# One-core fp32 kernel of two transformer blocks: modulation tiles as row sums on VectorE, exponentials moved behind splits and copies, part of an output projection inside the attention, four stores

## The chip, the cores and the metric

One Trainium2 chip; the program uses one of its cores. The metric is the device time of one execution in microseconds (us); lower is better.

## The reference

Two blocks run one after the other on 256 tokens of width 1024, all in fp32. The first has two layers: norm, an input projection, a convolution, a pooling mixer and a sparse attention, an output projection, a gated add of a side input. The second has two layers on the same tokens and, in its first layer, on 256 context tokens beside them (so 512 columns in layer 0, 256 in layer 1):

```python
mod = jax.nn.silu(c) @ w_ada[layer] + b_ada[layer]
sh1, sc1, g1, sh2, sc2, g2 = jnp.split(mod[:, None, :], 6, axis=-1)
modc = jax.nn.silu(c_ctx) @ w_ada[layer] + b_ada[layer]
...
u = modulate(rmsnorm_2(x, norm_mix_g[layer]), sh1, sc1) @ w_in[layer]
...
gla_lat, gla_ctx = gla_mixer(lat[:6], cpar[:6], rope, ...)
...
x = x + g1 * (jnp.concatenate([gla_lat, sc_lat, na_lat], axis=-1) @ w_out[layer])
h = modulate(rmsnorm_2(x, norm_ffn_g[layer]), sh2, sc2)
x = x + g2 * conv_ffn(h, ffn_w_up[layer], ffn_conv_w[layer], ffn_conv_b[layer], ffn_w_down[layer])
```

The modulation (mod and modc) is a product of two vectors, one for the tokens and one for the context, with a 1024 x 6144 matrix in each layer. It needs nothing but the inputs and can be computed at any time before its use.

## The kernel before, in words

The engines are TensorE (PE), VectorE (DVE), ScalarE (ACT), GpSimd (POOL) and SyncE (SP). Each runs its own instruction list, written out by hand, and waits on semaphores for the others.

**Weights.** All weights come as units of 128 x 1024 (512 KB) in the order that `stream()` writes. SP (line 434) loads them into a ring of four slots, RAWB; a slot is loaded again when its unit has been used up. An fp32 product is made of three products of operands split in a high and a low part: ACT copies a unit to WHI (line 1299, the helper through which every ACT instruction goes), DVE subtracts it from the unit to get WLO (line 1832). The split ring has three slots and runs two units ahead (AHEAD). `rest()` and `split_to()` are the places in the ACT and DVE lists where the next split stands. The activations are split too, into NHI and NLO.

**A tile** is 128 output channels: `fm` issues 8 slabs of three matmuls (lines 561 to 563) over 512 or 256 columns. `native` tiles (line 577) skip the split and multiply RAWB in fp32; in block 1 these are the tiles from NATIVE_FROM on, which stand beside its attention. `tm` units (lines 622 to 624) make token-major values V, copied from PSUM by ACT's `values`.

**Block 1** (0 to 400 us): per layer, values, tile 0, then tiles 1 to 22. DVE's `divide` (line 1887) scales a tile by the token norm, ACT adds the bias into Z, PE rotates (line 813), DVE applies the ropes (lines 2007 to 2012).

**Block 2**: per layer an input projection of 17 tiles and 8 value units, in the order 4 tiles, 4 value units, 13 tiles; beside it ropes and gates (GQ: exponential and logarithm on ACT; line 2475 on DVE), cumulative sums on PE (line 1080) behind tile 6, `cross_exponentials` on ACT at tile 8, the gated mixer's matmuls. Then a softmax attention by items (one pair of heads and 128 queries each): scores (line 1256), row maximum on DVE, exponential on ACT, transposes (line 736), values (line 1265). Then the output projection (8 tiles), statistics (line 697), `modulate` on DVE (GM, TB and NLO), the feed-forward: 44 tiles up, 8 tiles of three units down.

**The modulation** is cut in 24 tiles of 512 outputs, four units each, 12 for each layer. A "row" tile is computed by PE (`rows`, line 531, into a bank of 32 partitions), copied by ACT, turned into columns by four small matmuls (`columns`, line 542) and biased by DVE. A "dot" tile is computed by DVE alone (`dot`, line 1924): one instruction multiplies a unit with the broadcast vector CREP and sums along the row, per column of the modulation; units of tiles that also serve the context need two. Before, tiles 0 to 10 are rows: 0 to 3 in block 1 (ROWS1), 4 beside block 2's first tiles (ROWS2), 5 to 9 in layer 0's attention (BESIDE_ROWS), 10 behind the output projection's statistics; tiles 11 to 23 are dots in layer 0's feed-forward.

## Time and profile before

| what | value |
|---|---|
| median of 3 runs | 1489.95 us (1489.83 to 1494.48) |
| profiled execution | 1486.99 us, its span 1485.2 us |
| PE busy | 1402.2 us (94%) |
| VectorE busy | 987.8 us (67%) |
| ScalarE busy | 710.4 us (48%) |
| block 1 | 0 to some 400 us |
| block 2, layer 0; layer 1 | to 1061 us; to 1485 us |

Busy time is the time in which an engine executes an instruction. A timeline row gives start, length, engine, line, operation, what is written and read, how many instructions, and in brackets the idle time before it and what ended it.
### The profile page before, as it was taken

To read this page: it belongs to the slowest core of one execution; us is meant where nothing else is said; L and a number is where in the kernel's file an instruction comes from. 1 tells how busy PE (TensorE), PEld (TensorE's weight loads), DVE (VectorE), ACT (ScalarE), POOL (GpSimd) and SP (SyncE) were. 2 spreads that over 40 slices of the span, in tenths; PEclk is the share of its full clock that TensorE was granted. 3 is DMA by queue.
4 is the path that set the end of the run, shared out by engine and by line. 5 is a ranking of instruction groups with operands and counts; after the bars stand their busy time and mean duration, and the time that the engine had idled before them with its cause. 6 is when DMAs were issued, how large, how long until landed. Compare 5 with 4: busy or idle time off the path is not lost.

```text
span 1485.2 us, 22067 instructions
## 1 busy us (share of the span) xinstructions
PE 1402.2 (94%) x8641; PEld 1201.1 (81%) x8641; DVE 987.8 (67%) x1907; ACT 710.4 (48%) x1195; POOL 47.4 (3%) x66
## 2 busy tenths in 40 slices
PE   6999998998999999999999999999899988899997
PEld 4777897778977886577888888888788867899997
DVE  5597685977743385645798897665533655788854
ACT  5537565366534632633444444312344636566642
POOL 0000000000000012000000000000000210000000
PEclk9999999999999999998999999999899999999998
DMA  6633556334452221642345445567233331365552
GB/s 242 227 131 125 159 184 201 129 100 159 140 168 85 67 95 53 230 168 100 128 156 169 158 156 175 172 221 243 96 112 100 105 99 56 128 196 177 183 185 81
DMA packets 61752, 217.48 MB, mean 146 GB/s; under 512 B 6960, under 2 KB 9008, under 8 KB 61392
## 3 DMA queue, kind: packets, MB, share of 16 engines
q1 hardware_dynamic: 59152, 205.55, 42.1%
q0 software_dynamic: 2352, 10.52, 2.1%
q8 instruction: 69, 1.13, 0.3%
q14 instruction: 35, 0.29, 0.1%
q10 hardware_dynamic: 144, 0.00, 0.0%
HBM read 214.99 MB, written 1.05 MB: 145 GB/s over the span
## 4 chain that ended last, share of the span: by engine, by line
PE 80%; DVE 8%; ACT 7%; issue 3%; DMA 1%; DVEq 0%; ACTq 0%
PE bank L561 19%; PE bank L563 19%; PE bank L562 19%; PE bank L577 3%; ACT WHI L1299 2%; DVE WLO L1832 2%; PE bank L1137 1%; ACT L1299 1%; PE bank L622 1%; PE bank L623 1%; PE bank L624 1%; PE bank L531 1%; PE bank L736 1%; PE bank L599 1%; PE bank L1265 1%
## 5 line engine op out<-in xcount | busy, mean ns | idle before, releaser
L1832 DVE TENSOR_TENSOR WLO<-RAWB,WHI 128x1024 fp32r<-128x1024 f32 (+1 forms) x280 | 333.5, 1193 | 271.5 <-ACT WHI L1299 270.3
L561 PE MATMUL bank<-NHI,WHI 128*128 128x256 f32 (+1 forms) x1440 | 481.7, 335 | 15.8 <-DVE WLO L1832 8.6
L562 PE MATMUL bank<-NLO,WHI 128*128 128x256 f32 (+1 forms) x1440 | 474.0, 329 | 0.0
L563 PE MATMUL bank<-NHI,WLO 128*128 128x256 f32 (+1 forms) x1440 | 474.0, 329 | 0.0
L1299 ACT ACTIVATE WHI<-RAWB 128x1024 fp32r<-128x1024 f32 (+1 forms) x280 | 287.5, 1029 | 194.7 <-PE bank L563 131.5
L561 PEld LDWEIGHTS bank<-NHI,WHI 128*128 128x128 f32 x1440 | 275.7, 191 | 51.9 <-issue 14.7
L562 PEld LDWEIGHTS bank<-NLO,WHI 128*128 128x128 f32 x1440 | 275.9, 192 | 25.5 <-issue 2.2
L563 PEld LDWEIGHTS bank<-NHI,WLO 128*128 128x128 f32 x1440 | 275.5, 191 | 24.2
L1299 ACT ACTIVATE CF<-bank,PRM 128x512 f32<-128x512 f32 (+1 forms) x88 | 59.1, 671 | 178.7 <-PE bank L563 175.9
L561 PE MATMUL bank<-HHI,WHI 128*128 128x512 f32 (+1 forms) x352 | 119.3, 339 | 0.0
L563 PE MATMUL bank<-HHI,WLO 128*128 128x512 f32 (+1 forms) x352 | 119.2, 339 | 0.0
L562 PE MATMUL bank<-HLO,WHI 128*128 128x512 f32 (+1 forms) x352 | 119.2, 339 | 0.0
L1924 DVE CUSTOM_DVE_ANT_0 DP<-RAWB,CREP,PRM 128x1024 f32<-128x1024 f32 x72 | 92.3, 1282 | 3.5
L2559 DVE SCALAR_TENSOR_TENSOR CF<-bank,PRM,CF 128x510 f32<-128x510 f32 (+1 forms) x88 | 54.1, 615 | 50.7 <-ACT CF L1299 49.2
L577 PE MATMUL bank<-Y,RAWB 128*128 128x256 f32 x320 | 75.1, 389 | 0.0
L561 PEld LDWEIGHTS bank<-HHI,WHI 128*128 128x128 f32 x352 | 66.3, 188 | 8.3 <-DVE WLO L1832 0.2
L562 PEld LDWEIGHTS bank<-HLO,WHI 128*128 128x128 f32 x352 | 66.3, 188 | 8.1
L563 PEld LDWEIGHTS bank<-HHI,WLO 128*128 128x128 f32 x352 | 66.3, 188 | 8.1
L1299 ACT ACTIVATE L<-L,ST 128x256 f32<-128x256 f32 (+2 forms) x100 | 50.2, 518 | 39.3 <-DVE ST L1942 16.4
L577 PEld LDWEIGHTS bank<-Y,RAWB 128*128 128x128 f32 x320 | 60.6, 193 | 9.8 <-issue 1.7
L1299 ACT ACTIVATE ZB<-bank 128x512 f32<-128x512 f32 (+1 forms) x34 | 17.7, 520 | 95.0 <-PE bank L563 94.9
L622 PE MATMUL bank<-WHI,NHI 128*128 128x384 f32 (+1 forms) x128 | 47.9, 375 | 12.4 <-DVE WLO L1832 9.3
(319 smaller groups left out, 1928.4 us busy)
## 6 DMA issues: line engine op xcount, KB each, us to landing
RAWB<-in_ws SPq DMA_DIRECT2D x364, 512.0 KB, 3.4
RAWB<-in_ws SPq DMA_DIRECT2D x32, 384.0 KB, 3.5
NB<-in_nab POOLq DMA_DIRECT2D x12, 256.0 KB, 3.7
K<-in_c POOLq DMA_DIRECT2D x2, 896.0 KB, 4.7
K<-in_c POOLq DMA_DIRECT2D x1, 1344.0 KB, 7.9
X<-in_xt SPq DMA_DIRECT2D x4, 256.0 KB, 5.8
X<-in_xt POOLq DMA_DIRECT2D x1, 1024.0 KB, 6.5
CREP<-in_crep POOLq DMA_DIRECT2D x1, 1024.0 KB, 5.0
```

Of the source, the lines that this page charges most:

```text
L531: ins = nc.tensor.matmul(bank[b][g:g + 32, :], CV2[:, s, 8 - 2 * at:40 - 2 * at], RAWB[:, u % RAW, (s % 2) * 512:(s % 2 + 1) * 512], start ...
L561: nc.tensor.matmul(o, hi[:, w], xh, start=(i == 0), stop=False)
L562: nc.tensor.matmul(o, hi[:, w], xl, start=False, stop=False)
L563: ins = nc.tensor.matmul(o, lo[:, w], xh, start=False, stop=(i == slabs - 1))
L577: ins = nc.tensor.matmul(bank[b][:, 0:T], RAWB[:, u % RAW, s * P:(s + 1) * P], Y1[:, s, :], start=(s == 0), stop=(s == KS - 1))
L599: nc.tensor.matmul(o, hi[:, w], xh, start=(i == 0), stop=False)
L622: nc.tensor.matmul(o, xh, hi[:, c], start=(s == 0), stop=False)
L623: nc.tensor.matmul(o, xl, hi[:, c], start=False, stop=False)
L1299: return nc.scalar.activation(out, in_, func, **kw)
L1832: V.tensor_tensor(WLO[:, k % SPL, 0:w], RAWB[:, u % RAW, 0:w], WHI[:, k % SPL, 0:w].bitcast(F32), ALU.subtract).then_inc(S("lo_ready"), 1)
L1924: V.tensor_tensor_reduce(out=DP[:], in0=RAWB[:, u % RAW, :], in1=CREP[:, c, :], scale=1.0, scalar=prm_col(f"bada{l}", at), op0=ALU.mult, o ...
L2559: V.scalar_tensor_tensor(y[:, :, 1:], b[:, :, :-1], prm_col(f"fw{l}", j), y[:, :, 1:], ALU.mult, ALU.add).then_inc(S("dve_chain"), 1)
```

## The change

- Block 1: the two kb tiles are native too; the row units of tile 1 go to tile 2, and the division of tile 2 stands ahead of the split there.
- Modulation tiles 5 to 10 become dots. Twenty of their units go beside layer 0's input projection, in the numbers of DOTS_PROJ behind each tile or value unit, with a broadcast vector and a scratch tile of their own (CREP1, DP1); the other four shift the rest. The rows, copies, columns and additions of these tiles go.
- ACT copies the second half of the values and makes one more split before the exponential of the gates, and takes the logarithm a tile later; it makes one more split before `cross_exponentials`.
- Five of the eight slabs of the output projection's first tile are issued inside the softmax attention, in bank 3 (FIRST_OUT_AT).
- `modulate` computes GM before the statistics, and scales and splits by halves of 256 columns.
- The result is stored in four pieces.

```diff
-NATIVE_FROM = Z1["pin"]
+NATIVE_FROM = Z1["kb"]
...
-ROWS1 = (1, 4, 7, 10)
+ROWS1 = (2, 4, 7, 10)
...
-BESIDE_ROWS = 5
 ROWS2 = (0, 2)
-DOT_TILES = range(11, 24)
+FIRST_OUT_AT = ({7: (0,), 8: (1,), 9: (2,), 10: (3,), 11: (4,)}, {6: (0, 1), 7: (2, 3), 8: (4,)})
+DOT_TILES = range(5, 24)
+DOTS_FIRST = 20
+DOTS_PROJ = (1, 1, 1, 2, 2, 1, 2, 2, 2, 2, 2, 2)
 DOTS_UP = [m for m in range(5, 2 * FT) if m % 3]
-DOTS_DOWN = (4, 4, 4, 4, 4, 4, 2, 0)
+DOTS_DOWN = (5, 5, 5, 5, 4, 4, 2, 0)
...
+            dots(DOTS_PROJ[i] if l == 0 else 0)
             rows(2 if l == 0 and i in ROWS2 else 0)
-        add([2 * VW] * 4 + [UNIT] * (NZ2 - NFIRST))
-        rows(BESIDE_ROWS * ROW_U if l == 0 else 0)
+        for j, width in enumerate([2 * VW] * 4 + [UNIT] * (NZ2 - NFIRST)):
+            add([width])
+            dots(DOTS_PROJ[NFIRST + j] if l == 0 and NFIRST + j < len(DOTS_PROJ) else 0)
...
-            sp.wait_ge(S("x_new"), KS * (DEPTH + 2))
-            sp.dma_start(out, X[:, :, 0:T]).then_inc(S("stored"), 16)
-            sp.wait_ge(S("stored"), 16)
+            for k in range(0, KS, 2):
+                sp.wait_ge(S("x_new"), KS * (DEPTH + 1) + k + 2)
+                sp.dma_start(out[:, k:k + 2, :], X[:, k:k + 2, 0:T]).then_inc(S("stored"), 16)
+            sp.wait_ge(S("stored"), 16 * KS // 2)
...
+                if l == 0:
+                    pool.dma_start(CREP1[:], crep).then_inc(S("ld_crep"), 16)
...
+                if l == 0:
+                    pool.wait_ge(S("dot_summed"), DOTTED[DOTS_FIRST])
...
+                first_unit = []
+
+                def first_out(s):
+
+                    if s == 0:
+                        pe.wait_ge(*held[3])
+                        first_unit.append(unit())
+                    (hi, lo), (xh, xl) = first_unit[0], rhs(s)
+                    w, o = slice(s * P, (s + 1) * P), bank[3][:, 0:n]
+                    nc.tensor.matmul(o, hi[:, w], xh, start=(s == 0), stop=False)
+                    nc.tensor.matmul(o, hi[:, w], xl, start=False, stop=False)
+                    return nc.tensor.matmul(o, lo[:, w], xh, start=False, stop=(s == KS - 1))
+
                 def end_of_gated(i):
 
                     if i == 0:
                         output_means()
                     if i == 2:
                         output_scales()
-                    h = i - 3
-                    if uc and 0 <= h < 2 * BESIDE_ROWS:
-                        rows(3, 4 * (h % 2), 4 * (h % 2) + 4, h // 2, BESIDE_ROWS)
+                    if i == min(FIRST_OUT_AT[l]):
+                        pe.wait_ge(S("y_split"), me.nth("y_split", 5))
+                    for s in FIRST_OUT_AT[l].get(i, ()):
+                        first_out(s)
...
+                me.from_bank_3()
+                me.next_tile()
                 attention(items2(uc), score2, L2, lambda e: (4 + e, 0), pv2, uc, end_of_gated)
-                pe.wait_ge(S("y_split"), me.nth("y_split", 5))
-                me.from_bank_0()
+                for s in range(5, KS):
+                    pe.wait_ge(S("y_split"), me.nth("y_split"))
+                    ins = first_out(s)
+                ins.then_inc(S("unit_done"), 1)
+                read_by(3, "wo_freed")
                 for m in range(KS):
-                    fm(KS, n, rhs, "wo_freed", "y_split" if m == 0 else None, 5)
-                    if uc and m == 1:
-                        columns(3, BESIDE_ROWS)
+                    if m > 0:
+                        fm(KS, n, rhs, "wo_freed")
                     stats_behind(m, n, SQ2)
-                if uc:
-                    rows(5)
                 spread_scales("r_tok", "r_spread", n // P)
-                held[4] = (S("t_ready"), me.nth("t_ready", KS))
+                held[4] = (S("t_ready"), me.nth("t_ready", KS * seqs))
                 fm_side_by_side(AHEAD, n, rhs, "up_freed", "x_split")
...
+                    A(CREP1[:], CREP1[:], ACT.Silu).then_inc(S("crep_ready"), 1)
...
+                values(1)
+                split_to(me.u + 1 + AHEAD)
                 act.wait_ge(S("act_chain"), me.nth("act_chain", 4))
                 A(GTA, GTA, ACT.Exp, scale=-1.0).then_inc(S("act_chain"), 1)
-                act.wait_ge(S("act_chain"), me.nth("act_chain"))
-                A(GTA, GTA, ACT.Ln, bias=1.0).then_inc(S("gln_ready"), 1)
-                values(1)
                 for i in range(NFIRST, NZ2):
                     tile(i)
+                    if i == NFIRST:
+                        split_to(me.u + 1 + AHEAD)
+                        act.wait_ge(S("act_chain"), me.nth("act_chain"))
+                        A(GTA, GTA, ACT.Ln, bias=1.0).then_inc(S("gln_ready"), 1)
                     if i == 6:
                         fold_last_heads()
                     if i == 7:
@@ -1736,6 +1767,7 @@
                             act.wait_ge(S("b_ready"), me.nth("b_ready"))
                             A(BG[:, j, :], bank[4 + j][:]).then_inc(S("b_copied"), 1)
                     if i == 8:
+                        split_to(me.u + 1 + AHEAD)
                         cross_exponentials()
...
+                    if t == 2:
+                        divide(l, 2)
...
-                        divide(l, 2)
...
+                stats(n)
+
+                def scaled(s, c):
+
+                    w = slice(c * T, (c + 1) * T)
+                    V.scalar_tensor_tensor(TB2[:, s, w], X[:, s, w], GM[:, s, c:c + 1], bank[4][:, w],
+                                           ALU.mult, ALU.mult).then_inc(S("t_ready"), 1)
+
+                def low(s, c):
+
+                    w = slice(c * T, (c + 1) * T)
+                    dve.wait_ge(S("xh_ready"), me.nth("xh_ready"))
+                    dve.wait_ge(S("t_ready"), me.nth("t_ready"))
+                    return V.scalar_tensor_tensor(NLO[:, s, w], TB2[:, s, w], MOD[:, l, shift + s, c:c + 1],
+                                                  NHI[:, s, w].bitcast(F32), ALU.add, ALU.subtract)
+
                 for s in range(KS + 1):
                     if s in rests:
                         rest()
-                    for c in range(n // T):
-                        w = slice(c * T, (c + 1) * T)
-                        if s < KS:
-                            ins = V.scalar_tensor_tensor(TB2[:, s, w], X[:, s, w], GM[:, s, c:c + 1], bank[4][:, w], ALU.mult, ALU.mult)
                     if s < KS:
-                        ins.then_inc(S("t_ready"), 1)
+                        scaled(s, 0)
                     if s >= 1:
-                        dve.wait_ge(S("xh_ready"), me.nth("xh_ready"))
-                        dve.wait_ge(S("t_ready"), me.nth("t_ready"))
-                        for c in range(n // T):
-                            w = slice(c * T, (c + 1) * T)
-                            ins = V.scalar_tensor_tensor(NLO[:, s - 1, w], TB2[:, s - 1, w], MOD[:, l, shift + s - 1, c:c + 1],
-                                                         NHI[:, s - 1, w].bitcast(F32), ALU.add, ALU.subtract)
+                        for c in range(seqs):
+                            ins = low(s - 1, c)
                         ins.then_inc(S("x_split"), 1)
-
-            def residual(l, n, gate, units, sq, dots=(), beside=None):
+                    if s < KS and seqs == 2:
+                        scaled(s, 1)
...
+                def dots_beside(j):
+
+                    for _ in range(DOTS_PROJ[j] if l == 0 and j < len(DOTS_PROJ) else 0):
+                        dot()
+
                 for i in range(NFIRST):
                     rest()
+                    dots_beside(i)
                 if l == 0:
                     modulation(7)
                 for u in range(4):
                     rest()
+                    dots_beside(NFIRST + u)
                     if u == 1:
                         dve.wait_ge(S("ld_c2"), 16 * 2 * (l + 1))
                         for t in range(3):
                             rope(t)
                 for i in range(NFIRST, NZ2):
                     rest()
+                    dots_beside(4 + i)
+                    if l == 0 and i == 8:
+                        dve.wait_ge(S("dot_summed"), DOTTED[DOTS_FIRST])
```

Three places where the order moves. ACT's list in block 2, layer 0, from the last gate copies on (GQ are the gates, V the values, ZB a tile's copy), before:

```order
L1299 ACTIVATE GQ<-bank 128x2x192 x2
L1299 ACTIVATE WHI<-RAWB 128x1024
L1299 ACT_TABLE_LOAD
L1299 ACTIVATE GQ<-GQ 128x1536
L1299 ACT_TABLE_LOAD
L1299 ACTIVATE GQ<-GQ 128x1536
L1299 ACTIVATE V<-bank 128x384 x4
L1299 ACTIVATE WHI<-RAWB 128x1024
L1299 ACTIVATE ZB<-bank 128x512
L1299 ACTIVATE WHI<-RAWB 128x1024
```

and after:

```order
L1326 ACTIVATE GQ<-bank 128x2x192 x2
L1326 ACTIVATE WHI<-RAWB 128x1024
L1326 ACTIVATE V<-bank 128x384 x4
L1326 ACTIVATE WHI<-RAWB 128x1024
L1326 ACT_TABLE_LOAD
L1326 ACTIVATE GQ<-GQ 128x1536
L1326 ACTIVATE ZB<-bank 128x512
L1326 ACTIVATE WHI<-RAWB 128x1024
L1326 ACT_TABLE_LOAD
L1326 ACTIVATE GQ<-GQ 128x1536
L1326 ACTIVATE ZB<-bank 128x512
```

The four copies of V and a split stand ahead of the first table load, and a tile's copy and a split between the two exponential passes.

DVE's list in the same projection, two tiles of it, before:

```order
L2306 TENSOR_TENSOR ZB<-ZB,K 128x256
L2309 TENSOR_TENSOR ZB<-ZB,AM 128x256
L1832 TENSOR_TENSOR WLO<-RAWB,WHI 128x1024 x4
L2475 SCALAR_TENSOR_TENSOR GQ<-bank,GQ 128x2x192 x4
L1832 TENSOR_TENSOR WLO<-RAWB,WHI 128x1024 x3
L2332 COPY MR<-BK 128x16
L2333 COPY MR<-BK 128x2
```

and after (two units stand beside each tile; ISA rows that read RAWB are the row sums, those of 128x1 the read of their result):

```order
L1953 ISA DP,MOD<-RAWB,CREP,PRM 128x1024
L1953 ISA MOD 128x1
L1953 ISA DP,MOD<-RAWB,CREP,PRM 128x1024
L1953 ISA MOD 128x1
L2522 SCALAR_TENSOR_TENSOR GQ<-bank,GQ 128x2x192 x4
L1860 TENSOR_TENSOR WLO<-RAWB,WHI 128x1024
L1953 ISA DP,MOD<-RAWB,CREP,PRM 128x1024
L1953 ISA MOD 128x1
```

Where splits stood alone (four, the gates, three), four row sums stand between each two of them, and the gates (GQ) stand behind all that came before.

PE's list in layer 0's softmax attention, two items of it, before:

```order
L531 MATMUL bank<-RAWB,CV 32x512 x4
L736 MATMUL bank<-CST,L 128x128 x8
L1265 MATMUL bank<-PT,V 64x128 x8
L1256 MATMUL bank<-ZB 128x512 x2
L531 MATMUL bank<-RAWB,CV 32x512 x4
L736 MATMUL bank<-CST,L 128x128 x4
L1265 MATMUL bank<-PT,V 64x128 x8
L1256 MATMUL bank<-ZB 128x512 x2
L531 MATMUL bank<-RAWB,CV 32x512 x4
```

and after:

```order
L749 MATMUL bank<-CST,L 128x128 x8
L1292 MATMUL bank<-PT,V 64x128 x8
L1283 MATMUL bank<-ZB 128x512 x2
L1265 MATMUL bank<-NHI,WHI 128x512
L1266 MATMUL bank<-NLO,WHI 128x512
L1267 MATMUL bank<-NHI,WLO 128x512
L749 MATMUL bank<-CST,L 128x128 x4
L1292 MATMUL bank<-PT,V 64x128 x8
L1283 MATMUL bank<-ZB 128x512 x2
L1265 MATMUL bank<-NHI,WHI 128x512
```

The row matmuls between scores and transposes are gone, and a slab of the output projection's first tile stands in their place.

## Rows read from the trace of the kernel before

**Rows 1.** The page: busy us (share), instructions.

```profile
PE 1402.2 (94%) x8641; PEld 1201.1 (81%) x8641; DVE 987.8 (67%) x1907; ACT 710.4 (48%) x1195; POOL 47.4 (3%) x66
```

**Rows 2.** Timelines (start, length; idle before, releaser): block 1, layer 0, second projection tile.

```profile
44.74 0.42 DVE L1887 TENSOR_TENSOR Z<-bank,MS 128x256 f32<-128x256 f32 x1
...
45.76 0.70 PE L813 MATMUL bank<-Z,K 128*128 128x512 f32 x1 [2.31 <-ACT Z L1299]
```

**Rows 3.** The same place in layer 1, and the busy times around it.

```profile
231.49 1.06 ACT L1299 ACTIVATE WHI<-RAWB 128x1024 fp32r<-128x1024 f32 x1 [3.97 <-DMA RAWB<-in_ws]
...
236.03 1.22 PE L813 MATMUL bank<-Z,K 128*128 128x512 f32 x1 [3.51 <-ACT Z L1299]
...
232.00:240.00 8.00, 4.49 (x20) 3.25 (x19) 4.06 (x7) 4.87 (x8) 0.00 (x0) 0.79 0.51 169
```

**Rows 4.** By stretch, busy us (count): PE, PEld, DVE, ACT, POOL; PEclk, DMA, GB/s.

```profile
66.00:112.00 46.00, 43.91 (x273) 35.91 (x271) 42.00 (x124) 19.08 (x46) 0.92 (x1) 0.96 0.44 150
...
760.00:780.00 20.00, 20.00 (x90) 16.58 (x89) 18.52 (x25) 7.66 (x11) 0.00 (x0) 1.00 0.51 160
1300.00:1320.00 20.00, 20.00 (x169) 20.00 (x168) 17.31 (x30) 12.88 (x22) 0.00 (x0) 1.00 0.63 202
```

**Rows 5.** PE behind ScalarE's Exp, Ln: waits (total, times, longest), layer 0's row, stretch.

```profile
PE bank L561 <- ACT V L1299: 7.1, 2, 3.5
...
468.13 0.80 PE L561 MATMUL bank<-NHI,WHI 128*128 128x512 f32 x1 [3.54 <-ACT V L1299]
...
468.00:472.00 4.00, 3.87 (x10) 3.07 (x11) 1.23 (x1) 2.16 (x5) 0.00 (x0) 0.58 0.00 0
```

**Rows 6.** Block 2, layer 1: PE behind the cross exponentials, and the stretch.

```profile
1166.19 0.35 PE L561 MATMUL bank<-NHI,WHI 128*128 128x256 f32 x1 [3.62 <-DVE WLO L1832]
...
1162.00:1172.00 10.00, 6.38 (x41) 6.20 (x41) 7.14 (x19) 8.78 (x14) 0.00 (x0) 0.83 0.32 106
```

**Rows 7.** Line 1924 alone; unit loads (KB, us to landing); layer 0's input projection.

```profile
L1924 DVE CUSTOM_DVE_ANT_0 DP<-RAWB,CREP,PRM x72: 1276/1284/1287, 729.0 to 1045.1; 128x1024 f32<-128x1024 f32 x72
...
RAWB<-in_ws SPq DMA_DIRECT2D x364, 512.0 KB, 3.4
...
400.00:440.00 40.00, 38.27 (x204) 32.23 (x204) 19.34 (x40) 16.51 (x26) 3.51 (x5) 1.00 0.43 140
440.00:480.00 40.00, 36.46 (x188) 32.25 (x187) 12.54 (x21) 15.45 (x20) 0.00 (x0) 0.96 0.30 100
```

**Rows 8.** VectorE and PE in that projection: a weight split, the gates, the sums.

```profile
439.34 0.96 DVE L1832 TENSOR_TENSOR WLO<-RAWB,WHI 128x768 fp32r<-128x768 f32 x1 [5.53 <-ACT WHI L1299]
...
478.13 1.95 DVE L2475 SCALAR_TENSOR_TENSOR GQ<-bank,GQ 128x384 f32<-128x384 f32 x4
...
486.10 1.04 PE L1080 MATMUL bank<-K,GQ 128*128 128x256 f32 x5
```

**Rows 9.** Attention of layer 0, then of layer 1: PE's row matmuls, and stretches.

```profile
L531 PE MATMUL bank<-RAWB,CV 128*32 128x512 f32 x80 | 12.7, 604 | 0.0
...
600.00:638.00 38.00, 38.00 (x327) 19.16 (x325) 23.26 (x84) 24.34 (x66) 1.42 (x2) 1.00 0.83 287
...
1226.00:1230.00 4.00, 4.00 (x28) 3.03 (x26) 3.27 (x11) 3.59 (x10) 0.00 (x0) 0.61 0.06 23
```

**Rows 10.** The first tile of the output projection: PE's start, VectorE's last operand.

```profile
638.01 0.50 PE L561 MATMUL bank<-NHI,WHI 128*128 128x512 f32 x1
...
639.48 0.69 DVE L2539 TENSOR_TENSOR NLO<-OY,NHI 128x512 fp32r<-128x512 f32 x1 [5.03 <-ACT NHI L1299]
```

**Rows 11.** Between projection and feed-forward, layer 0.

```profile
686.14 3.48 PE L531 MATMUL bank<-RAWB,CV 128*32 128x512 f32 x16
...
707.78 0.50 PE L542 MATMUL bank<-CST,ROWS 128*128 128x2 f32 x4
```

**Rows 12.** The end: last scaling of VectorE; the store's GB/s in 1470 to 1486, 0.4 us each.

```profile
1476.73 3.22 DVE L2582 SCALAR_TENSOR_TENSOR X<-X,PRM,bank 128x256 f32<-128x256 f32 x8 [1.39 <-PE bank L785]
...
GB/s 0 0 0 0 0 0 0 0 0 0 0 20 0 0 0 0 0 0 0 0 0 0 0 0 0 0 0 0 269 346 351 346 346 348 348 269 0 0 0 0
```

60 lines of the change are left out of this document (27 added, 33 removed).

## Prediction

> **What bounds it now.** I read the page first: PE is busy 1402.2 of the 1485.2 us [rows 1], so all engines but PE matter only where PE waits for them, and at most 83 us can come from waits; the rest must come from PE work removed. Then PE's timeline with its idle times, place by place, and at each the engine named there; then stretches, for how full VectorE is where work is put on it, and for the granted clock. VectorE is the engine to watch: nearly full in the feed-forward of layer 0 (18.52 of 20 us, while PE never waits [rows 4]), almost empty in that layer's input projection (19.34 and 12.54 of 40 us [rows 7]). From the stretches without a PE gap I price a tile: 90 matmuls in 20 us make a 24-matmul tile 5.3 to 5.4 us with 512 columns, 169 make it 2.9 us with 256 [rows 4]. All terms are in profiled time (span 1485.2, run 1486.99 us); the median of the runs is 2.96 us above that, and I add this at the end.
>
> **Block 1, the head of each layer: -5.6.** At its second projection tile PE waits for a division on VectorE that stands behind a weight split, which waits for ScalarE, which waited for a weight unit's DMA: 2.31 us in layer 0 [rows 2], 3.51 in layer 1 after a DMA wait of 3.97 [rows 3]. The row units of tile 1 go to tile 2 and the division goes ahead of the split, so both waits should go. Layer 1's stretch also shows a clock of 0.79 over 8 us, 1.7 us lost [rows 3], most of it in the tile after the wait; I take back 1.3 of it and 0.5 of the slow rotation. The row matmuls, 1.0 us in each layer (two units, eight matmul records; 80 take 12.7 us in the attention [rows 9], so 1.3, of which 0.3 overlaps what follows), no longer hide under a wait: +1.0 twice. So -1.3 in layer 0 and -4.3 in layer 1. If a new wait for the row units' slots comes at tile 2, only -3.
>
> **The two kb tiles unsplit: -3.1.** A native tile takes PE some 0.6 us more than a split one (3.6 against 2.9 by their neighbours), +1.2 a layer, and frees VectorE of two splits of 1.22 us. VectorE is busy 42.00 of 46 us there while PE loses 2.1 us and some clock [rows 4], so I count what is freed: -2.0 in layer 0, -1.1 in layer 1. Bounds: +2.4 (nothing comes of it), -4.6.
>
> **Row sums beside layer 0's input projection: +2.4.** 20 units with two columns are 40 instructions of 1.284 us [rows 7], 1.32 apart, 51 to 53 us of VectorE. Up to tile 3 they fit in its idle time. From the split at 439.34 [rows 8] the queue is full: 13 units (34.3), seven splits (three of 0.96, four of 1.22: 7.8), the ropes (3.9), a bias (0.2) and the gates (1.95 [rows 8]) end at about 487.5, against 480.1 now. PE would come to the sums that read those gates at 486.10 [rows 8] less what the next part gives (3.54 + 1.64), at 480.9, and so waits some 6.6 us in all, part of it earlier, at the gates' banks and at splits. Half a microsecond of gaps in tile 11 goes. Waits of this size cost clock: the tile after 3.54 us ran at 0.58 for 4 us, 1.7 us lost [rows 5]; I put 1.4 here. So -5.2 + 6.6 + 1.4 - 0.4 = **+2.4**, with layer 0's gain from the Exp and Ln order in it. Behind the full queue stand GpSimd's clearing of QX and the K2 load behind one more 1 MB load; both have over 25 us until used. Bounds: -4 if splits are never late, +6 if they are late at each tile. The other eight instructions go to feed-forward tiles whose VectorE has 1.5 us in 20 free [rows 4]: 4 x 1.32 us over 40 tiles, nothing; without that cover up to +5.
>
> **Rows out of layer 0's attention: -1.6.** The five row tiles hold PE for 12.7 us there [rows 9], and PE is busy 38.00 of 38 us. But the order transpose, values, next scores, row maximum, exponential is a chain of its own, ending each item at most 1.4 us ahead of PE; without the rows it comes out only some 1.7 us shorter. Bounds: 0 (+3 if the clock falls) and -4.
>
> **Five slabs of the first output tile inside the attention: -2.5 in layer 0, 0 in layer 1.** PE starts that tile at 638.01, and the last operand is ready at 640.17 (639.48 + 0.69) [rows 10]. Of 5.4 us, only the slabs 5 to 7 remain, the last starting at about +2.2 and ending at +2.9: -2.5. The 15 matmuls of 0.23 us fit where the 12.7 us of rows were.
>
> **Columns, statistics, operand order: -3.3.** The two column groups go (five matmuls and four; four take 0.50 us [rows 11]): -1.1. The 3.48 us of row matmuls behind the statistics [rows 11] cover a Newton iteration on VectorE, which starts when the statistics end and comes out from under them: between 0 (it is as long as they are) and -3.5 (nothing waits for it); I take -0.8, near the first, as the next matmuls read its result. The gain product ahead of the statistics and the half-wise scaling: -0.6 before the feed-forward of layer 0, -0.8 in layer 1.
>
> **Layer 1's values and splits ahead of the exponentials: -7.3.** PE waits twice for the value copies behind Exp and Ln with their table loads, 7.1 us in all, 3.5 each [rows 5]. With the copies ahead layer 1's wait goes, 3.5 and 1.4 of clock: -4.9. The wait of 3.62 us behind the cross exponentials, in a stretch at clock 0.83 [rows 6], gets one more split tile (2.9 us of PE) in hand: -2.9, less 0.5 as that split now delays the exponentials: -2.4. Late next would be Ln, which the gates need five tiles later.
>
> **Stores: -2.3.** The last scaling ends at 1479.95, the kernel at 1485.2 [rows 12]: 5.25 us for 1 MB, of which 3.0 move bytes at some 350 GB/s [rows 12]; a last quarter needs 0.75 and the same 2.2 of start and end. The Trainium skill ("DMA: Bandwidth & Descriptors", "Anatomy of one DMA — SWDGE (gpsimd) path") puts a fixed cost of about 2.0 us on each DMA and so speaks against small ones; by it a 256 KB store takes 2.6 us, and four in a row would lose 6 if they queued. The row's own split, 2.2 and 3.0, agrees with the fixed part; I take it as overlapped, since scalings free a quarter every 0.8 us. By the rule without overlap the stores would be +4 and the total 1473.
>
> **Sum.** -5.6 - 3.1 + 2.4 - 1.6 - 2.5 - 3.3 - 7.3 - 2.3 = -23.3: 1463.7 profiled, **1466.7** on the median.
>
> **Rivals.**
> 1. **The ring exposes each row sum (slower).** A row-sum unit lies in one of the four weight slots until VectorE has summed it, and a load lands 3.4 us after its issue [rows 7]. If the slot of each of the 13 later units came free only as the next split wants it, each would cost that 3.4 us: +44, 1508. It becomes slower than before once VectorE's queue slips 23.3 us, that is 1.8 us per unit. Against: each tile brings three units in 6.4 us, and each load has 4.5 us or more from its slot's release to its use; 287 GB/s flowed in the attention. Chance 0.04.
> 2. **The clock takes half (smaller gain).** With rows in the attention the clock stays 1.00; layer 1's attention, without them, shows 0.61 from 1226 [rows 9], nearly the lower of TensorE's two levels. If layer 0's goes the same way over some 10 us (+4), the waits in the input projection cost 3 more of clock and the native tiles give nothing (+3): -13, 1477. The Trainium skill ("TensorE: Matmul & The Clock Gate", "HAM oscillation — how this bites in real kernels") says that a TensorE idle between bursts falls back to 1.2 GHz, a rule that speaks against taking filler matmuls out. By that rule, the trace agrees for layer 1's attention; for layer 0, whose PE stays nearly full with slabs in it, no row decides. Chance 0.22.
> 3. **VectorE keeps up (larger gain).** If the 6.6 us of waits and their clock don't appear, because row sums slip into idle time before 439, -8 more: 1459. Chance 0.12.
> 4. **Nothing to measure.** Gains on PE come back as waits at the next split; 1490 within 0.3%. Against: six of the waits end on orders that the change plainly alters. Chance 0.04.
>
> **Numbers.** The forecast has 0.58. Measurement tells 0.3%, 4.5 us. Its own bounds give 1461 to 1472; with rivals 2 and 3 inside, 1458 to 1478 leaves out rivals 1 and 4 and a little of each edge. Faster 0.92, same 0.04, slower 0.04.
>
> **What would show it.** PE busy falls by some 20 us (12.7 + 3.5 + 1.1 of rows and columns, 2.1 of clock, less 2.4 of native tiles). The waits of PE for V and Z are gone; a new one, for gates or splits, stands at about 480 to 490. VectorE is nearly full from 430 to 485. PEclk near 450 to 480 is 0.9 or above, and 1.00 in layer 0's attention; if it is below 0.8 there, rival 2. The last projection tile of layer 0 starts some 25 us late if rival 1 holds. The last store lands under 3 us after its issue; at 5 or more, the store term fails. A span of block 1 not 7 us shorter would make the first two terms wrong.

## The result, and the profile after

| what | before | changed |
|---|---|---|
| median | 1489.89 us (4 runs, 1486.07 to 1494.48) | 1468.44 us (4 runs, 1467.59 to 1475.27) |
| profiled run, its span | 1486.99 us, 1485.2 us | 1468.17 us, 1466.4 us |
| PE busy | 1402.2 us | 1389.6 us |
| VectorE busy | 987.8 us | 1041.9 us |

The ratio of the two is 0.987, with a 95% interval of 0.9845 to 0.9895: the change is faster by 1.3%, clear of the 0.3% that a measurement can tell. The profiled span fell by 18.8 us; 23.3 were forecast.

The busy times on the page of the changed kernel answer to [rows 1]:

```profile
PE 1389.6 (95%) x8497; PEld 1196.2 (82%) x8497; DVE 1041.9 (71%) x1993; ACT 709.3 (48%) x1191; POOL 48.0 (3%) x67
```

VectorE took on 54 us of work and PE gave off 12.6, not the 20 forecast (the terms written beside that 20 add up to 17.0). A slow clock counts as work here: the first matmul of one and the same tile is busy for 0.80 us in [rows 5], in a stretch at 0.58, and for 0.39 us at 464.30 below. The changed kernel's PE in block 1, at the second and third tile (timelines of layer 0, then layer 1) and the stretches behind the waits answer to [rows 2, 3]:

```profile
36.24 0.41 PE L837 MATMUL bank<-CST,Z 128*128 128x128 f32 x2 [3.58 <-ACT Z L1326]
...
45.53 0.59 PE L826 MATMUL bank<-Z,K 128*128 128x512 f32 x1
...
49.35 1.99 PE L544 MATMUL bank<-RAWB,CV 128*32 128x512 f32 x8
...
38.00:42.00 4.00, 4.00 (x26) 3.59 (x28) 0.68 (x2) 0.55 (x1) 0.00 (x0) 0.70 0.82 257
...
223.26 0.41 PE L837 MATMUL bank<-CST,Z 128*128 128x128 f32 x2 [1.99 <-ACT Z L1326]
...
226.00:230.00 4.00, 4.00 (x25) 3.02 (x25) 1.20 (x2) 0.83 (x3) 0.00 (x0) 0.74 0.68 214
```

The waits for Z at the second tile (2.31 and 3.51 us) are gone. But the wait one tile earlier, in which the row matmuls ran, is now 3.58 us without them (before, 2.20 and 0.32 with 1.06 us of rows between), and the tile behind it runs at a clock of 0.70; in layer 1 0.74, after 1.99 us. The row matmuls of tile 4 also take longer in layer 0, 1.99 us for eight records instead of 1.06. In layer 0 all this takes back more than the second tile gave.

Layer 0's input projection in the changed kernel: VectorE's list (timeline) where its queue fills and where the gates end it, ScalarE's logarithm, PE at the row units (with the weight load of their second unit), at the gates' second bank, at the first tile behind the values, and at the sums; then the whole stretch. It answers to [rows 5, 7, 8]:

```profile
436.07 0.96 DVE L1860 TENSOR_TENSOR WLO<-RAWB,WHI 128x768 fp32r<-128x768 f32 x1 [3.00 <-ACT WHI L1326]
...
481.61 1.95 DVE L2522 SCALAR_TENSOR_TENSOR GQ<-bank,GQ 128x384 f32<-128x384 f32 x4
...
475.87 1.49 ACT L1326 ACTIVATE GQ<-GQ 128x1536 f32<-128x1536 f32 x1
...
420.30 1.05 PE L544 MATMUL bank<-RAWB,CV 128*32 128x512 f32 x4 [0.80 <-DMA RAWB<-in_ws]
...
421.44 0.14 PEld L544 LDWEIGHTS bank<-RAWB,CV 128*32 128x32 f32 x4 [1.01 <-DMA RAWB<-in_ws]
...
452.37 0.91 PE L1054 MATMUL bank<-WG,ZB 17*128 17x192 f32 x4 [0.69 <-DVE AM L2342]
...
464.30 0.39 PE L574 MATMUL bank<-NHI,WHI 128*128 128x512 f32 x1
...
483.61 0.76 PE L1093 MATMUL bank<-K,GQ 128*128 128x256 f32 x2 [2.79 <-DVE GQ L2522]
...
436.00:484.00 48.00, 44.52 (x219) 39.15 (x218) 46.17 (x74) 20.10 (x27) 0.00 (x0) 0.96 0.73 232
```

VectorE is busy 46.17 of the 48 us from 436 to 484. From the split at 436.07 to the end of the gates at 483.56 are 47.5 us; the working had 48.2. The wait of 3.54 us for V is gone (no idle time at 464.30), and three new ones stand there, with a fourth of 1.01 us inside the row matmuls. PE comes to the sums at 480.82.

In layer 0's softmax attention (PE's timeline, its waits for the exponentials from 598 to 640 as total, times and longest, and the stretch), then behind it (the operands of the first tile, the statistics and the feed-forward's start), answering to [rows 9 to 11]:

```profile
604.23 0.89 PE L749 MATMUL bank<-CST,L 128*128 128x128 f32 x4 [1.34 <-ACT PT L1326]
...
PE bank L749 <- ACT PT L1326: 4.6, 4, 1.8
...
602.00:638.00 36.00, 30.68 (x245) 20.08 (x244) 22.10 (x78) 25.53 (x66) 0.43 (x1) 1.00 0.05 16
...
636.25 0.49 PE L1265 MATMUL bank<-NHI,WHI 128*128 128x512 f32 x1 [0.56 <-DVE NLO L2586]
...
680.54 2.07 PE L798 MATMUL bank<-CST,GR 128*128 128x128 f32 x8 [1.74 <-DVE GR L1882]
...
684.93 0.76 PE L612 MATMUL bank<-NHI,WHI 128*128 128x512 f32 x1 [2.32 <-DVE NLO L2292]
```

PE now waits for the attention's exponentials, its clock stays 1.00, and the DMA share falls from 0.83 to 0.05. In layer 1 the waits behind the exponentials (PE) answer to [rows 5, 6], and the end (scaling, the four stores with KB and median us to landing) to [rows 12]:

```profile
1123.49 0.39 PE L574 MATMUL bank<-NHI,WHI 128*128 128x256 f32 x1 [0.58 <-ACT V L1326]
...
1133.24 1.14 PE L1093 MATMUL bank<-K,GQ 128*128 128x256 f32 x5 [0.84 <-DVE GQ L2522]
...
1154.88 0.35 PE L574 MATMUL bank<-NHI,WHI 128*128 128x256 f32 x1 [2.02 <-DVE WLO L1860]
...
1460.15 3.22 DVE L2626 SCALAR_TENSOR_TENSOR X<-X,PRM,bank 128x256 f32<-128x256 f32 x8 [0.89 <-PE bank L798]
...
out_x<-X SPq DMA_DIRECT2D x4, 256.0 KB, 2.6
```

**The ledger.** The same PE instruction was looked up in both traces, and the shift of its start read stage by stage; the shifts add up to the 18.8 us. The last row is counted from VectorE's last scaling. Where an experiment gives a number of its own, it stands in brackets.

| stage | forecast | measured |
|---|---|---|
| first values (not touched) | 0 | -0.4 |
| head of block 1, layer 0, to behind the row matmuls of tile 4 | -1.3 | +1.0 |
| native kb tiles, layer 0 | -2.0 | -2.9 (e5: -1.8) |
| head of block 1, layer 1 | -4.3 | -2.1 |
| native kb tiles, layer 1 | -1.1 | -1.2 (e5: -1.2) |
| end of block 1 | 0 | +0.4 |
| layer 0's input projection to the attention | +2.4 | +4.1 |
| layer 0's attention, first tile, columns | -4.7 | -6.2 |
| statistics, GM, halves, second columns | -1.9 | -3.1 |
| layer 1: start and value units | -0.8 | +1.1 |
| layer 1: values, sums, cross exponentials | -7.3 | -6.0 |
| layer 1: gated part, attention, feed-forward | 0 | -1.3 |
| stores | -2.3 | -2.2 (e6: -2.2) |

Of the 6.2 us of layer 0's attention, first tile and columns, 2.8 are the attention itself (in the kernel before from 600.85 to 638.01, now from 599.71 to 634.03, with the slabs in it), 2.6 the first tile and 0.8 the columns.

### The profile page after: what moved, and what is told of

Its sections match the earlier page's. It is cut to its first block, busy times and chain, and to the rows that moved or that the text cites. A ratio compares the mean times of both kernels' runs of the same rounds, so it can differ in the third digit from the quotient of the medians.

```text
span 1466.4 us, 21897 instructions
## 1 busy us (share of the span) xinstructions
PE 1389.6 (95%) x8497; PEld 1196.2 (82%) x8497; DVE 1041.9 (71%) x1993; ACT 709.3 (48%) x1191; POOL 48.0 (3%) x67
## 4 chain that ended last, share of the span: by engine, by line
PE 81%; DVE 9%; ACT 7%; issue 3%; DMA 1%; DVEq 0%; ACTq 0%
PE bank L574 20%; PE bank L576 19%; PE bank L575 19%; PE bank L590 5%; DVE DP L1953 2%; ACT WHI L1326 2%; PE bank L1150 1%; DVE WLO L1860 1%; ACT L1326 1%; PE bank L635 1%; DVE NLO L2292 1%; ACT NHI L1326 1%; PE bank L1093 1%; PE bank L636 1%; PE bank L637 1%
## 5 line engine op out<-in xcount | busy, mean ns | idle before, releaser
L574 PE MATMUL bank<-NHI,WHI 128*128 128x256 f32 (+1 forms) x1392 | 464.6, 334 | 8.2 <-DVE WLO L1860 6.8
L575 PE MATMUL bank<-NLO,WHI 128*128 128x256 f32 (+1 forms) x1392 | 458.9, 330 | 0.0
L576 PE MATMUL bank<-NHI,WLO 128*128 128x256 f32 (+1 forms) x1392 | 458.7, 330 | 0.0
L574 PEld LDWEIGHTS bank<-NHI,WHI 128*128 128x128 f32 x1392 | 265.7, 191 | 44.7 <-issue 13.6
L575 PEld LDWEIGHTS bank<-NLO,WHI 128*128 128x128 f32 x1392 | 265.9, 191 | 24.7 <-issue 1.4
L576 PEld LDWEIGHTS bank<-NHI,WLO 128*128 128x128 f32 x1392 | 265.8, 191 | 23.3
L1953 DVE CUSTOM_DVE_ANT_0 DP<-RAWB,CREP,PRM 128x1024 f32<-128x1024 f32 x120 | 153.9, 1282 | 7.2 <-DMA RAWB<-in_ws 1.3
L590 PE MATMUL bank<-Y,RAWB 128*128 128x256 f32 x384 | 88.2, 383 | 0.0
L2603 DVE SCALAR_TENSOR_TENSOR CF<-bank,PRM,CF 128x510 f32<-128x510 f32 (+1 forms) x88 | 54.1, 614 | 44.2 <-ACT CF L1326 42.8
L590 PEld LDWEIGHTS bank<-Y,RAWB 128*128 128x128 f32 x384 | 71.5, 190 | 11.8 <-issue 2.7
L2606 DVE SCALAR_TENSOR_TENSOR CF<-bank,PRM,CF 128x510 f32<-128x510 f32 (+1 forms) x88 | 54.2, 616 | 3.1
```

Of the source, the lines that this page charges most:

```text
L574: nc.tensor.matmul(o, hi[:, w], xh, start=(i == 0), stop=False)
L575: nc.tensor.matmul(o, hi[:, w], xl, start=False, stop=False)
L576: ins = nc.tensor.matmul(o, lo[:, w], xh, start=False, stop=(i == slabs - 1))
L590: ins = nc.tensor.matmul(bank[b][:, 0:T], RAWB[:, u % RAW, s * P:(s + 1) * P], Y1[:, s, :], start=(s == 0), stop=(s == KS - 1))
L1953: V.tensor_tensor_reduce(out=prod[:], in0=RAWB[:, u % RAW, :], in1=rep[:, c, :], scale=1.0, scalar=prm_col(f"bada{l}", at), op0=ALU.mult, ...
L2603: V.scalar_tensor_tensor(y[:, :, 1:], b[:, :, :-1], prm_col(f"fw{l}", j), y[:, :, 1:], ALU.mult, ALU.add).then_inc(S("dve_chain"), 1)
```

## The experiments

**e1, gates ahead of the row sums** (of the tile whose row sums stood ahead of them):

```diff
-                    dots_beside(4 + i)
...
                     if i == 5:
                         dve.wait_ge(S("gln_ready"), me.nth("gln_ready"))
...
+                    dots_beside(4 + i)
```

> The changed kernel with one move: on VectorE, in layer 0's and layer 1's input projection, the gates stand ahead of the four row sums of that tile instead of behind them. Theory (VectorE's full queue makes PE wait for the gates at the cumulative sums): ScalarE's logarithm ends at 477.4, the gates then at some 479.4, before PE arrives at 480.8; the gap of 2.79 us ahead of the sums goes and with it the slow clock behind it (1.8 us): span 1462 instead of 1466.4. Rival (the same VectorE work has to be done anyway, the wait only changes place): the gap comes back at a later tile or split, span 1466.

Span 1467.2 us, median 1468.43. VectorE in this kernel (timeline):

```profile
477.45 1.95 DVE L2519 SCALAR_TENSOR_TENSOR GQ<-bank,GQ 128x384 f32<-128x384 f32 x4 [0.48 <-ACT GQ L1326]
```

The gates end at 479.4, and PE starts the sums without a wait; from the tile before to the end of the sums it gained 4.7 us on the changed kernel. So the cause of that wait is shown. The span gained nothing: 2.2 us were lost again between 593 and 613 and the rest further on, by clock. In the changed kernel's trace and in this one's, the stretches at the end of the gated part (their waits there are no longer here than there):

```profile
590.60:594.60 4.00, 2.37 (x20) 1.66 (x19) 2.88 (x13) 3.96 (x8) 0.00 (x0) 0.50 0.00 0
594.60:598.60 4.00, 3.70 (x41) 3.32 (x38) 2.54 (x8) 2.21 (x7) 0.00 (x0) 0.73 0.00 0
```

```profile
582.90:586.90 4.00, 3.11 (x17) 1.56 (x16) 1.32 (x5) 3.69 (x6) 0.00 (x0) 0.67 0.00 0
586.90:590.90 4.00, 3.12 (x24) 2.40 (x26) 3.51 (x17) 3.96 (x9) 0.00 (x0) 0.50 0.00 0
590.90:594.90 4.00, 4.00 (x36) 3.51 (x32) 1.96 (x3) 1.48 (x5) 0.00 (x0) 0.55 0.00 0
```

By the granted clock that is the worth of some 7 us at half clock in the one (6.2 in these rows, and the four us ahead of them are at 0.92) and of some 10 in the other, over the same work.

**e2, the row units of tile 1 back** (`ROWS1 = (1, 4, 7, 10)`):

> The changed kernel with ROWS1 = (1, 4, 7, 10) again, the division of tile 2 still ahead of the split. Theory (the row matmuls of tile 1 filled PE's wait for Z and so kept the clock): in both layers of block 1 the clock over the next tile is 1.00 again instead of 0.70 and 0.74, some 2.1 us less in each; and the old waits for Z of 2.31 and 3.51 us stay away, since the division no longer stands behind the split: span 1462. Rival (the two row units in the ring make the weight split wait for its DMA, and that is what PE waited for): the waits of 2 to 3.5 us come back, span 1466 to 1469.

Span 1463.9 us, median 1465.98. PE and the stretch in layer 0 (layer 1 alike):

```profile
35.30 1.07 PE L544 MATMUL bank<-RAWB,CV 128*32 128x512 f32 x8 [2.19 <-ACT CV L1326]
...
43.70 1.10 PE L826 MATMUL bank<-Z,K 128*128 128x512 f32 x2 [0.20 <-DVE RT L2036]
...
38.00:42.00 4.00, 4.00 (x36) 4.00 (x35) 1.22 (x2) 1.14 (x3) 0.00 (x0) 1.00 0.71 242
```

The clock is 1.00, the waits for Z stay away: counted to behind the row matmuls of tile 4, 2.6 us gained in layer 0 and 2.3 in layer 1. Of each, 1.0 is the row matmuls' own time, which lies in the wait again, and 1.2 and 1.0 are the slow clock (0.70 and 0.74 over 4 us); in layer 0 the row matmuls of tile 4 are also 0.8 us shorter (1.19 us against 1.99). The theory holds; the earlier division alone removed the waits, and moving the rows only cost. Of the 5.8 us that it led by at 456, 3.2 were given back by 593: PE came earlier to the sums and waited 4.33 us there, and the end of the gated part ran at half clock for longer, as in e1.

**e3, both halves scaled before the split of the slab ahead, in layer 1:**

```diff
                     if s < KS:
                         scaled(s, 0)
+                        if rests and seqs == 2:
+                            scaled(s, 1)
...
-                    if s < KS and seqs == 2:
+                    if s < KS and seqs == 2 and not rests:
                         scaled(s, 1)
```

> The changed kernel with one move: ahead of layer 1's input projection VectorE scales both halves of a slab before it splits the slab ahead, as before the change. Theory (the halves delay ScalarE's operand and so the weight split behind it, by 0.66 us for each of two splits, in a stretch that VectorE bounds): the gaps of 0.35 and 0.58 us at the value units go, PE starts 0.7 us later and ends the value units 0.7 to 1.9 us earlier: span 1464.5 to 1465.7. Rival (the chain of VectorE ends as before, its order is indifferent): span 1466.4, or 1467 as the start is later.

Span 1468.6 us, median 1470.27. PE starts that layer 0.55 us later and ends the value units 0.6 us earlier than the changed kernel, measured against the shift it had before; the gap of 0.35 us is gone, the one of 0.58 stays. The direction is the theory's, the size is below its range. The span is longer by clock elsewhere, which says nothing on the edit.

**e4, without the projection's row sums** (DOT_TILES from 10, DOTS_FIRST and DOTS_PROJ zero, tiles 5 to 9 skipped):

> The changed kernel without the 20 row-sum units beside layer 0's input projection: modulation tiles 5 to 9 are left out altogether (their modulation is zero), all else stays. It measures what these row sums cost PE. Theory (they cost it by VectorE's queue and by loads of the ring, in waits and in clock): the gaps of 0.80, 0.69 and 2.79 us and the slow clock behind each go, and PE reaches the gated attention some 9 us earlier: span 1457.5. Rival (the waits there come from ScalarE and the clock alone): at most 3 us less, span 1463.5 or more.

Span 1455.5 us, median 1460.79. The gaps at 420, 452 and 484 are gone. From the start of block 2 to the first tile behind the sums it gains 9.8 us, and keeps it. So VectorE's queue and the ring's loads, together, cost all that; ScalarE's order leaves no wait of its own there. Counted from the start of block 2, PE comes to the sums after 71.0 us here, against 76.3 in the kernel before: the whole 5.2 us that the working had for ScalarE's order. In the changed kernel it comes after 76.3 us again.

**e5, the kb tiles split again** (`NATIVE_FROM = Z1["pin"]`):

> The changed kernel with the two kb tiles of each layer of block 1 split again (NATIVE_FROM at pin). Theory (the two native tiles relieve VectorE where PE waits for it): the stretch between the rows of tile 4 and the last native tiles grows by 2.9 us in layer 0 and by 1.2 us in layer 1, with the waits for the transposes' operand L back: span 1470.5 against 1466.4. Rival (that gain came from the earlier division and rows, and the native tiles cost PE 1.2 us a layer for nothing): span 1464 to 1466.

Span 1469.5 us, median 1472.58. The waits for L are back at both places, here layer 0's:

```profile
95.67 0.53 PE L876 MATMUL bank<-CST,L 128*128 128x128 f32 x2 [1.39 <-ACT L L1326]
```

Counted from behind the row matmuls of tile 4, the stretch with the native tiles grows by 1.8 us in layer 0 and 1.2 in layer 1: the native tiles are worth 3.0, and the waits that they take away are the named ones. The theory's 1.2 is met. Its 2.9 was read against the kernel before, which ran at a clock of 0.59 from 96 to 100; here, behind the same waits, the clock is 1.00 there. Whether 1.1 of the 2.9 us, this clock, belong to the native tiles is open: e8 and e9, with the same block 1 as the kernel before, are slow there too (0.62 and 0.57).

**e6, one store:**

> The changed kernel with the one store of 1 MB at its end. Theory (only the last quarter's bytes are exposed, the fixed part overlaps): from the end of the last scaling to the end of the program 5.2 us again instead of some 2.8, all else equal: +2.4, span 1468.8. Rival (four stores pay the fixed part each, as the Trainium skill's page DMA: Bandwidth & Descriptors, section Anatomy of one DMA, would have it if they queue): the stretch is no longer than with four stores.

Span 1473.1 us, median 1473.07. SP issues at 1467.88, the last scaling ends at 1467.85, the program at 1473.1: 5.25 us, against 3.0 (1463.37 to 1466.4) with four. The four are worth 2.2 us. They don't queue: each takes 2.6 us to land, and all four lie within 5.35 us (1461.05 to 1466.4). The other 4.5 us of this span come from stretches that the edit doesn't touch: a slow clock near 209 and 590, and near 453 a wait for the gates' bank of 2.23 us instead of 0.69, with a slow clock behind it.

**e7, all slabs of the first tile behind the attention** (FIRST_OUT_AT empty, the loop behind the attention over all eight):

> The changed kernel with all eight slabs of the output projection's first tile behind the softmax attention, in both layers. Theory (the slabs fill PE's idle time there): the attention of layer 0 gets no shorter, and the tile behind it 2.5 to 3.4 us longer; in layer 1 0 to 1.8 us longer: span 1469 to 1471.6. Rival (the slabs delay the attention's own chain, as PE has them ahead of transposes): the attention shortens by as much, span 1466. Second rival (without slabs PE idles more and the clock falls in layer 0's attention): 1473 or more.

Span 1469.1 us, median 1470.6. Up to 621 the attention is 1.0 us shorter than with slabs, so they do delay it a little; from there to the feed-forward layer 0 loses 5.5 us, 1.5 of them by a slow clock (0.64 and 0.51 between 622 and 626) and 0.7 by a longer wait. At its end the attention without slabs is 1.3 us longer than with them, and the tile behind it 2.6. So in this pair of traces the slabs are worth 3.9 us in layer 0 up to there, of which the clock's part may differ in another execution, and 0.3 less than nothing in layer 1's attention. Neither rival holds alone: of the first a quarter came, of the second the dip of the clock.

**e8, ScalarE's order alone, in the kernel before:**

> The kernel before with one part of the change: ScalarE copies the values and splits ahead of the gates' exponential, takes the logarithm behind the next tile's copy, and splits once more ahead of the cross exponentials. Theory (these waits are ScalarE's order alone, and VectorE has room in both layers): the two waits of 3.54 us go with 1.6 and 1.4 us of clock, the one of 3.62 us shrinks by 2.4 to 2.9: 12.5 us in all, span 1472.7 against 1485.2. Rival (the logarithm, now later, makes the gates late for the sums): a new wait of 1 to 3 us ahead of the sums in each layer, span 1475 to 1479.

Span 1477.4 us, median 1476.41. By 513 it is 5.7 us ahead in layer 0 (3.5 of wait, 0.4 of the next gap, the rest clock), and in layer 1 it gains another 7.1 up to the tile that had waited 3.62 us, as much as the changed kernel does. Its gates are late for the sums there, by 1.70 us: the rival is half right. Behind the 2.02 us that PE still waits one tile later 6.1 are left, in both kernels, and 4.9 behind the slow clock that follows here. But layer 0's lead fell from 3.8 at 599 to 1.3 at 683. In its attention PE waited for the row units:

```profile
617.02 1.05 PE L531 MATMUL bank<-RAWB,CV 128*32 128x512 f32 x4 [0.86 <-DMA RAWB<-in_ws]
```

The kernel before, in the same stretches, showed why, in the last but one column (DMA share), which I had not read, and in PE's weight loads (one row, and their waits for loads from 598 to 640: total, times, longest):

```profile
608.00:612.00 4.00, 4.00 (x30) 1.45 (x26) 3.50 (x12) 2.11 (x8) 0.00 (x0) 1.00 0.96 314
...
628.00:632.00 4.00, 4.00 (x36) 2.43 (x35) 2.62 (x12) 2.75 (x9) 0.00 (x0) 1.00 1.01 372
...
613.03 0.14 PEld L531 LDWEIGHTS bank<-RAWB,CV 128*32 128x32 f32 x4 [0.91 <-DMA RAWB<-in_ws]
...
PEld bank L531 <- DMA RAWB<-in_ws: 2.0, 4, 0.9
```

So in the kernel before the loads themselves cost 2.0 us of that attention, inside three of the ten groups of row matmuls (1.62, 2.10 and 1.50 us; the others take 1.06 to 1.08).

**e9, thin rows, in the kernel before** (128 of 512 columns multiplied, units loaded as before; three quarters of modulation tiles 5 to 9 are left out):

> The kernel before, in which the row matmuls of layer 0's attention multiply only the first 128 of their 512 columns; the weight units are loaded as before. It leaves out three quarters of modulation tiles 5 to 9. It tells PE's time from the loads' time in that attention. Theory (the loads of the 20 units bound it: DMA share 0.92 to 1.02 at 314 to 372 GB/s in most of 604 to 636, row matmuls stretched from 1.06 to 2.1 us): PE is freed of some 9 us, and the stretch from PE's first row matmul to the first projection tile, 37.2 us, shortens by 2 us at most. Rival (PE's row matmuls were the cost, and the attention's own chain is much shorter than I had): it shortens by 5 us or more, as in the changed kernel.

Span 1481.5 us, median 1484.02. PE's row matmuls (groups by form, 597 to 640) wait for loads as soon as they are short:

```profile
L532 PE MATMUL bank<-RAWB,CV 128*32 128x128 f32 x80 | 6.0, 285 | 2.4 <-DMA RAWB<-in_ws 2.4
```

Busy time fell by 6.7 us, and the attention by 2.6 only (34.6 us). Neither number is met, but the loads' theory is the nearer: PE waits 2.4 us for loads, and the stretch stays within 3 us of its old length. The loads are not all of it: PE also waits 1.2 us for exponentials here, and in the changed kernel, with no load in the way but five slabs put in, the same stretch is 34.3 us, with 4.6 us of such waits.

**e10, combined** (e1, e2, e3, and the ropes ahead of their value unit's row sums) and **e11, the changed kernel again**, on one chip with the kernel before (17 runs, median 1488.46):

```diff
-                    dots_beside(NFIRST + u)
                     if u == 1:
...
                             rope(t)
+                    dots_beside(NFIRST + u)
```

> The changed kernel with the gates ahead of the row sums, the row units of tile 1 back, the full-width order ahead of layer 1's input projection, and the ropes of layer 0's input projection ahead of that value unit's row sums. Theory (each removes its own wait, and the clock behind a wait varies by some us from place to place): by the parts -2.8 to -4.5 (gates), -3 to -5.8 (rows), -0.6 (order), -0.5 to -2 (ropes), less what a changed phase of the clock gives back: span 1456 to 1461, and by median 5 to 10 us under the changed kernel. Rival (the gains are given back by the clock later on, as in the first two experiments): within 3 us of the changed kernel.

> The changed kernel as it is, again, beside the combined one on the same chip. It shows how far executions of one program lie apart, and where in the trace. Theory (what differs is the clock behind waits, not the waits): the gaps of PE are the same to 0.1 us, and the span differs by up to some 3 us, all of it in stretches at half clock. Rival (waits themselves vary): gaps differ by over 0.5 us at several places.

The combined kernel: median 1460.24 us (5 runs, 1458.0 to 1462.15), ratio to before 0.9809 (0.9785 to 0.9833), span 1456.9. The changed one: 1469.46 us (6 runs, 1466.14 to 1473.28), ratio 0.9869 (0.9848 to 0.9891). So 9.2 us by the medians, and no run of one reaches a run of the other: the gains are kept. Its waits at 420 and 452 are gone; PE now comes 7.3 us earlier to the sums (473.56 against 480.82) and waits 1.70 us there.

e11's span is 1471.5 us, 5.1 more than the same program's first profile. Of 49 gaps over 0.25 us all but seven are the same to 0.1 us (span less PE's busy time is 78.0 us against 76.8), so waits vary too, at few places; at the sums it waits 4.37 us instead of 2.79, since it came earlier to a queue that ends at the same time. The rest is clock, here in the two traces over the same work, the changed kernel's first profile first:

```profile
610.50:614.50 4.00, 3.66 (x29) 2.85 (x30) 2.31 (x13) 2.61 (x9) 0.00 (x0) 1.00 0.00 0
```

```profile
612.00:616.00 4.00, 3.44 (x20) 2.78 (x20) 1.38 (x6) 2.86 (x10) 0.00 (x0) 0.57 0.00 0
```

The wait ahead, 1.83 us in one and 1.82 in the other, cost nothing in the first and 1.6 us of clock in the second. The theory holds for most of it; the size, 5 us, is above what I had written.

**e12, rows kept** (the kernel before with ScalarE's order, the native kb tiles, the division ahead with its rows left at tile 1, and four stores):

> The kernel before with only these parts of the change: ScalarE's order around the exponentials, the two native kb tiles, the division ahead of the split (row units left at tile 1) and the four stores. Modulation tiles 5 to 10 stay rows on PE, all eight slabs stay behind the attention, and the statistics and halves are as before. It tells whether moving tiles 5 to 10 to VectorE pays. By the runs so far: heads of block 1 some -2 and -5, native tiles -2.5, ScalarE's order -7.8 (with what layer 0's attention gives back), store -2.2: span 1466, so by itself the move (with the slabs, and with the row units at tile 1) was worth about nothing in the changed kernel, and is worth some 9 us in the combined one (1456.9), where its waits are repaired. Rival (the move pays as it stands): span 1470 or more. Second rival (the move costs): 1463 or less.

Span 1464.0 us, median 1465.53 (4 runs, 1463.18 to 1467.21), ratio 0.9847 (0.9807 to 0.9887). With four small parts of the change and without its main one, the kernel is no slower than the changed one (0.987 and 0.9869 in its two measurements), perhaps 3 us faster. The fairest comparison is e2, which has the row units at tile 1 as well: span 1463.9 and median 1465.98 us there, 1464.0 and 1465.53 here. So in the changed kernel the move of tiles 5 to 10, with the slabs and the operand order that came with it, paid nothing. Against this kernel the combined one loses 5.2 us in layer 0's input projection (up to 560) and wins 12.9 from there to the start of the feed-forward. By the medians it is 5.3 us faster, measured on two chips whose kernels before lie 0.3 us apart; what the move alone has of this, without slabs, statistics and operand order, was not measured.

## Why the prediction was right, and where its steps were off

The forecast, 1466.7 us, lies 1.7 below the median, in its range. The likeliest case came about, in its order of size; of the rivals none did. Part of the closeness is luck: in profiled time, in which the terms are, 23.3 us were forecast and 18.8 came; the before profile lay 2.9 under its median and the changed one 0.3, which gave 2.6 back; and the stages miss by up to 2.3 us, to both sides. Point by point:

- **Block 1, the heads (-5.6 forecast, -1.1 measured).** The step that failed is that the rows, taken out from under a wait, cost +1.0 and no more. They had kept PE at work in a wait for Z; without them the clock fell to 0.70 and 0.74 for 4 us. e2 shows it: 2.6 and 2.3 us in the two layers, of which 1.0 each was in the sum. The test set for it (block 1 at least 7 us shorter) failed, at 5.3.
- **Native tiles (-3.1; 3.0 by e5).** Right, mechanism and size. The ledger's 4.1 has 1.1 us of a slow clock in the kernel before, which was not in the sum and which e5 didn't bring back.
- **Row sums beside the projection (+2.4, +4.1).** The length of VectorE's queue was right to 0.7 us, and so was ScalarE's part (e4: 5.3 us, forecast 5.2). That PE came to the sums at 480.82, with 480.9 in the working, is chance: the working counts in the time of the kernel before, in which block 2 starts 5.3 us later. Counted from the start of block 2, the queue ended 1.3 us later than forecast and PE came 5.2 us later, no earlier than in the kernel before. The term that was mis-sized is the waits and their clock, 6.6 + 1.4 in the sum, 9.8 by e4, and their places. Against e4, 2.0 us are lost at the row matmuls, by waits of 0.80 and 1.01 for loads of the crowded ring, which were not in the sum at all, 3.1 around the wait for the gates' bank and 4.7 at the sums; a slow clock stands behind the last two (0.67 from 452 to 456, 0.57 from 484 to 488). e1 shows the queue, e4 the whole price. It was hidden in a net number: the projection gave 5 us by ScalarE's order at the same time.
- **The attention (-1.6 of -4.7; -2.8 of -6.2).** The chain that the forecast named is there: without the rows PE waits 4.6 us for exponentials. The step that failed is the reading of the state before: PE busy for 38 of 38 us was taken for PE's own work. 2.0 us of it are waits for loads, which only the weight load rows show, at a DMA share of up to 1.02, and e8 and e9 show that the loads hold this attention as soon as PE is faster. How the missing 1.2 us divide between loads and chain was not separated.
- **Slabs (-2.5 and 0; first tile -2.6), stores (-2.3, measured -2.2, e6 2.2), layer 1's values and cross exponentials (-7.3, -6.0).** Right. The 1.3 us missing in layer 1 are the gates' wait of 0.84, which I had named as late next, and the remaining 0.58 for V; e8, with this part of the change alone, has the same gain up to the last of these waits.
- **Layer 1's start and value units (-0.8, +1.1).** The start came 0.9 us earlier and the value units ended later. Of the 2.0 us lost in between, 1.1 are new waits of PE (0.35, 0.18 and 0.58); the order by halves costs 0.6 us at the stage's end (e3). So an early start was worth nothing here, which fits a chain on VectorE that bounds the stage; the rest of the loss is open.
- **Two sums.** PE busy was to fall by some 20 us, but the terms listed add up to 17.0. The 1508 us of the first rival is 1463.7 + 44, in profiled time; on the median it would be 1511.
- **The clock rival** did not come in the attention, at 1.00 with slabs in it, but came at the heads, where filler was taken from PE. Its place was wrong, not its mechanism: without the slabs the clock did fall in the attention, to 0.64 and 0.51 (e7). By the rule that I had cited from the Trainium skill ("TensorE: Matmul & The Clock Gate", "HAM oscillation — how this bites in real kernels"), that an idle TensorE falls back to 1.2 GHz, the trace agrees at the heads.

## What to carry to other kernels

Before work is taken out of a wait, look at what else keeps the engine busy there: filler that costs nothing in a wait may hold the clock, and it is cheaper to remove the wait first. A large transfer of work to an idle engine should be put behind the few instructions that somebody waits for: here the kernel with the transfer was no faster than the one without it, and 5 us faster once the gates and the ropes stood ahead of the row sums. Judge an edit by the shift of the same instruction on both sides of its stage, not by one span: two profiles of one program differed by 5 us.

## What the hardware showed that was not expected

The clock behind a wait is no fixed price. One program, with equal waits, ran the work behind a wait of 1.83 us at full clock in one execution and at 0.57 for 4 us in another; behind the waits near 590 the clock lost the worth of some 7 to 10 us at half speed. The kernel before spread over 1482.44 to 1495.57 us in 17 runs on one chip, the combined kernel, whose waits are fewer, over 1458.0 to 1462.15 in 5; that the waits make the difference is not shown, and 5 runs are few.

And a group of matmuls that waits within itself can show no idle time: eight row matmul records took 1.06 us at best and up to 2.10 in the kernel before, with PE busy throughout. The waits stand one engine over, on the rows of the weight loads: 0.91 us at 613.03, 2.0 in that attention.
